# A streaming encoder step on one core: high-weight products first in each tile, and six small moves beside it

## What is computed

```python
x = layer_norm(ALPHA * x + 0.5 * swiglu(x, w_in, w_out))       # two feed-forward parts per layer
# layer 0: S5 mixer. lambda-bar and B-bar from a, dt, b; h[t] = lb * h[t-1] + bb @ u[t]
y = einsum(c_re, hs_re) - einsum(c_im, hs_im) + d_skip * u       # "outputs" of the state space
y = gelu(y) @ w_glu; y = y[:D] * sigmoid(y[D:])
# layer 1: k, v = x @ w_kv (before the layer), q = x @ w_q, rotary on k and q, masked softmax(q k) v, @ w_o
x = layer_norm(ALPHA * x + y)
x = layer_norm(ALPHA * x + 0.5 * swiglu(x, w_in2, w_out2))
```

## Time and profile before

| | |
|---|---|
| time, median of 3 runs | 2318.58 us (2316.3 to 2318.84) |
| the profiled execution | 2318.47 us, its span 2316.7 us |
| PE busy | 97% of the span |
| DVE, ACT, POOL busy | 65%, 50%, 25% |

### The profile page before, as it was taken

How to read it: one execution, slowest core, us unless ns; L and a number is a source line. 1 busy time by engine, 2 the same in 40 slices (tenths; PEclk the granted TensorE clock), 3 DMA queues, 4 the chain that set the end, 5 groups by cost and what they waited for, 6 DMA issues and landing times.

```text
span 2316.7 us, 42670 instructions
## 1 busy us (share of the span) xinstructions
PE 2242.5 (97%) x17171; PEld 2202.2 (95%) x17171; DVE 1516.4 (65%) x2276; ACT 1153.7 (50%) x1939; POOL 572.5 (25%) x491
## 2 busy tenths in 40 slices
PE   8989999999998999999999999999999999999997
PEld 8988999999998998999999999999999999999997
DVE  6898768657788577444474575656687665475444
ACT  4434543565744558433364465555466564354332
POOL 2267401123211342211251123011352011132110
PEclk9999999999999999999999999999999999999998
DMA  9568675454765455555569655544556456455452
GB/s 252 167 194 234 194 218 179 121 171 139 215 213 173 137 166 155 182 151 150 146 201 284 191 162 169 155 121 138 152 156 183 131 149 189 115 153 169 143 157 79
DMA packets 705366, 391.13 MB, mean 169 GB/s; under 512 B 25001, under 2 KB 693138, under 8 KB 705170
## 3 DMA queue, kind: packets, MB, share of 16 engines
q1 hardware_dynamic: 662720, 332.44, 50.1%
q10 hardware_dynamic: 42450, 55.96, 7.3%
HBM read 366.53 MB, written 21.82 MB: 168 GB/s over the span
## 4 chain that ended last, share of the span: by engine, by line
PE 75%; DVE 8%; ACT 3%; issue 2%; POOL 2%; ACTq 0%; POOLq 0%; DVEq 0%
PE tile_ps L542 22%; PE tile_ps L543 22%; PE tile_ps L544 22%; DVE wl L520 2%; PE misc L1749 1%; PE misc L1729 1%; ACT wh L514 1%; PE misc L2109 1%; POOL zq L886 1%; PE misc L2134 1%; PE misc L2309 1%; DVE hs L1557 1%; PE misc L1746 1%; PE misc L2287 0%; DVE r L978 0%
## 5 line engine op out<-in xcount | busy, mean ns | idle before, releaser
L520 DVE TENSOR_TENSOR wl<-raw,wh 128x1024 fp32r<-128x1024 f32 (+1 forms) x640 | 796.0, 1244 | 443.4 <-ACT wh L514 441.5
L542 PE MATMUL tile_ps<-xh,wh 128*128 128x256 f32 (+1 forms) x3520 | 1050.5, 298 | 23.0 <-DVE wl L520 18.6
L543 PE MATMUL tile_ps<-xl,wh 128*128 128x256 f32 (+1 forms) x3520 | 1033.7, 294 | 0.0
L544 PE MATMUL tile_ps<-xh,wl 128*128 128x256 f32 (+1 forms) x3520 | 1033.6, 294 | 0.0
L514 ACT CAST wh<-raw 128x1024 fp32r<-128x1024 f32 (+1 forms) x640 | 655.2, 1025 | 733.4 <-PE tile_ps L544 723.8
L542 PEld LDWEIGHTS tile_ps<-xh,wh 128*128 128x128 f32 x3520 | 664.7, 189 | 31.3 <-issue 20.3
L543 PEld LDWEIGHTS tile_ps<-xl,wh 128*128 128x128 f32 x3520 | 664.7, 189 | 0.9
L544 PEld LDWEIGHTS tile_ps<-xh,wl 128*128 128x128 f32 x3520 | 664.2, 189 | 0.0
L730 POOL TENSOR_TENSOR hl<-hf,hh 128x256 fp32r<-128x256 f32 (+1 forms) x176 | 243.4, 1383 | 1271.4 <-ACT hh L638 1270.8
L542 PE MATMUL tile_ps<-hh,wh 128*128 128x320 f32 (+1 forms) x1472 | 442.3, 300 | 5.8 <-DVE wl L520 5.6
L543 PE MATMUL tile_ps<-hl,wh 128*128 128x320 f32 (+1 forms) x1472 | 433.5, 294 | 0.0
(11 more groups left out here) (301 smaller groups left out, 1767.2 us busy)
## 6 DMA issues: line engine op xcount, KB each, us to landing
raw<-in_ffn_w_in_dram SPq DMA_DIRECT2D x352, 512.0 KB, 3.9
raw<-in_ffn_w_out_dram SPq DMA_DIRECT2D x128, 448.0 KB, 3.6
raw<-in_ffn_w_out_dram SPq DMA_DIRECT2D x64, 512.0 KB, 3.9
raw<-in_ssm_w_glu_dram SPq DMA_DIRECT2D x32, 512.0 KB, 3.8
raw<-in_attn_w_kv_dram SPq DMA_DIRECT2D x32, 512.0 KB, 4.0
wt<-scr_w ACTq DMA_DIRECT2D x16, 512.0 KB, 4.8
cp<-scr_c ACTq DMA_DIRECT2D x16, 512.0 KB, 4.1
raw<-in_attn_w_q_dram SPq DMA_DIRECT2D x16, 512.0 KB, 3.9
```

The lines of the kernel that those rows point to most:

```text
L520: nc.vector.tensor_tensor(wl[n % WS][:, 0:k, :], raw[n % RAWS][:, 0:k, :], wh[n % WS][:, 0:k, :].bitcast(F32), ALU.subtract).then_inc(w_lo, 1)
L542: nc.tensor.matmul(o, wh[w][:, kk, :], xa, start=kk == 0, stop=False)
L543: nc.tensor.matmul(o, wh[w][:, kk, :], xb, start=False, stop=False)
L544: return nc.tensor.matmul(o, wl[w][:, kk, :], xa, start=False, stop=kk == ROWS[n] - 1)
```

## The change

Six edits. (1) PE opens a tile on `wh` alone, does all rows' products with high weights, then waits for `wl`, then does all rows with low weights; tiles that wait row by row for their input, and the two tiles taken together, keep the old order and wait for `wl` first. (2) The state-space outputs begin a step (a tile) later. (3) The second half of x is copied out of PSUM twice by ACT, to `r` and to `xh`; DVE has no part in it. (4) The powers of lambda begin 40 steps later in the tables' program. (5) The eight `skip` tiles are made by ACT. (6) K/V tiles come in another order, and four V tiles are emptied by DVE.

```diff
-KV_ORDER = "kvvvvkkvvvvkkkkk"
+KV_ORDER = "kvvvvkkkvvvvkkkk"
+V_BY_DVE = 8
...
-            pe.wait_ge(w_lo, n + 1)
+            pe.wait_ge(w_hi, n + 1)
...
         def pe_tile(pe, n, h, hi, lo, ready=None, have=0):
             pe_open(pe, n)
+            if ready is None:
+                for kk in range(ROWS[n]):
+                    pe_row_high(n, h, hi, lo, kk)
+                pe.wait_ge(w_lo, n + 1)
+                for kk in range(ROWS[n]):
+                    mm = pe_row_low(n, h, hi, kk)
+                mm.then_inc(tile_done, 1)
+                return
+            pe.wait_ge(w_lo, n + 1)
...
             pe_open(pe, n)
             pe_open(pe, n + 1)
+            pe.wait_ge(w_lo, n + 2)
...
                 wait(pe, s_r2, d)
+                wait(pe, xh_ready[1], X_IN + d)
...
-        def dve_second(dve):
-            for d in range(DT):
-                dve.wait_ge(s_tpx, d + 1)
-                nc.vector.tensor_copy(r[:, d, CS[1]], misc[:, 3, 0:NT[1]]).then_inc(s_r2, 1)
-                yield from idle(2)
-
         def act_second(act):
             for d in range(DT):
-                yield
-                act.wait_ge(s_r2, d + 1)
-                nc.scalar.copy(xh[1][:, d, :], r[:, d, CS[1]]).then_inc(xh_ready[1], 1)
-                yield
+                act.wait_ge(s_tpx, d + 1)
+                nc.scalar.copy(r[:, d, CS[1]], misc[:, 3, 0:NT[1]]).then_inc(s_r2, 1)
+                nc.scalar.copy(xh[1][:, d, :], misc[:, 3, 0:NT[1]]).then_inc(xh_ready[1], 1)
+                yield from idle(2)
...
             w0, w1 = (tmp[:, 15 + k].rearrange("p (a b) -> p a b", a=2) for k in range(2))
+            yield from idle(5 * DT)
...
-                        V.tensor_scalar(skip[dt % 2][:, :], ident[:, :], vec[:, 96 + dt:97 + dt], None, ALU.mult
-                                        ).then_inc(s_dd, 1)
...
                     inputs(dt, 0)
+                    wait(act, s_tb, 3 * (dt - 1))
+                    nc.scalar.activation(skip[dt % 2][:, :], ident[:, :], ACT.Identity,
+                                         scale=vec[:, 96 + dt:97 + dt]).then_inc(s_dd, 1)
...
         def outputs_at(h, grp):
-            return 12 + (grp + 1) * SCAN[h]
+            return 13 + (grp + 1) * SCAN[h]
...
-                else:
-                    act_v_copy(act, 0, j)
+                elif i < V_BY_DVE:
+                    act_v_copy(act, 0, j)
+                else:
+                    act_hi(act, FIRST["kv"] + i + WS)
...
-                    dve_lo(dve, v_tile(0, j) + WS)
+                    n = v_tile(0, j)
+                    if i >= V_BY_DVE:
+                        dve.wait_ge(tile_done, n + 1)
+                        nc.vector.tensor_copy(vT[:, j, 0:NT[0]], bank(n, 0)).then_inc(drained[n % PSS], 1)
+                    dve_lo(dve, n + WS)
```

More of the change, by code:

```diff
@@ L536, in pe_open, with pe_row_high, pe_row_low @@
                 pe_busy(ps[:, n % PSS, 0:P], BUSY_TILES[n])
-            pe.wait_ge(w_lo, n + 1)
-        def pe_row(n, h, hi, lo, kk):
[L540 to L544, removed]
+            pe.wait_ge(w_hi, n + 1)
+        def pe_row_high(n, h, hi, lo, kk):
+            o, w = ps[:, n % PSS, 0:NT[h]], n % WS
+            nc.tensor.matmul(o, wh[w][:, kk, :], hi[:, kk, 0:NT[h]], start=kk == 0, stop=False)
+            nc.tensor.matmul(o, wh[w][:, kk, :], lo[:, kk, 0:NT[h]], start=False, stop=False)
+        def pe_row_low(n, h, hi, kk):
+            return nc.tensor.matmul(ps[:, n % PSS, 0:NT[h]], wl[n % WS][:, kk, :], hi[:, kk, 0:NT[h]],
+                                    start=False, stop=kk == ROWS[n] - 1)
+        def pe_row(n, h, hi, lo, kk):
+            pe_row_high(n, h, hi, lo, kk)
+            return pe_row_low(n, h, hi, kk)
         def pe_tile(pe, n, h, hi, lo, ready=None, have=0):
             pe_open(pe, n)
+            if ready is None:
+                for kk in range(ROWS[n]):
+                    pe_row_high(n, h, hi, lo, kk)
+                pe.wait_ge(w_lo, n + 1)
[4 more added lines that the diff above has]
+            pe.wait_ge(w_lo, n + 1)
             for kk in range(ROWS[n]):
[L549 to L552, removed]
+                if kk == 0 and n in BUSY_ROWS:
+                    pe_busy(ps[:, n % PSS, 0:P], BUSY_ROWS[n])
+                pe.wait_ge(ready, have + kk + 1)
                 mm = pe_row(n, h, hi, lo, kk)
@@ L1136, in pool_second @@
                 yield
+                pool.wait_ge(s_r2, d + 1)
                 pool_lo(pool, 1, d, X_IN)
@@ L2779, in _ @@
                              paced(together(dve_tables(dve), dve_powers(dve)), TABLES))
-            beside = together(chained(dve_rest(dve), dve_lam(dve)), tables, chained(idle(SECOND), dve_second(dve)),
+            beside = together(chained(dve_rest(dve), dve_lam(dve)), tables,
                               chained(idle(LN0), dve_ln(dve, 0, 0), dve_s5(dve, 0)))
```

## The result

The changed kernel (the reordering and five moves beside it) took 2303.66 us (median of six runs, 2303.04 to 2304.83) against 2317.93 in the same comparison: a ratio of 0.9936 (95% interval 0.9923 to 0.9949), 14.3 us less. I had forecast 2292, 26 us less than before, in a range of 2279 to 2308. The sign and the range held; the gain that I forecast was nearly double the measured one.

What follows compares the result with a forecast made beforehand. PE, busy 97% of the span, was taken as the bound, so only its waits and slow clock could be won. Stretch gains of 16.3, 4.6, 0.75, 0.7, -0.8, 3.9 and 1.3 summed to 26.7 us: 2292 us, range 2279 to 2308.

Steps and rivals of the forecast that it cites:

- The wait for `r` and the slow clock behind it: Near 124:130: ACT copies x at once, so the waits (5.6 us with restarts) and half-pace clock (2.7 us) are won back.
- A fulfilled wait in a tile's middle: Inside each tile, before the low products: costs nothing; a rival (chance 0.05) had a bubble there, break-even at 46 ns a tile.
- 723:765: Half 1, within 600:765: DVE has 1.4 us idle of 42 and sheds nothing, so the end rule gains only 0.75 us.
- Costs at nothing: Mid-tile waits, copies and `skip` tiles on ACT, later powers beside POOL's `zq` adds, V copies on DVE: taken as 0 us.
- my own account: Whole kernel: the forecast's stretch-by-stretch sum, 26.7 us gained, 2292 us, own range 2283 to 2301; chance 0.60.
- rival A: Whole kernel: DVE bounds more, waits return later as `wl` mid-tile, `wh` or `cp`; gain 8 to 14 us; chance 0.22.
- 0:300: First stretch: `wl`, `r` and most `ebuf` waits clear, with slow clock and small gaps; 16.3 us gained.
- `ebuf` waits: Within 82:240: DVE sheds around 17 us, so the first four of five go, 4.0 us; 0.8 given back for POOL.
- A wait for `wl` that is shorter than the 1.81 us of high products vanishes if DVE is only late once: Any plain tile: the high products cover it; if DVE has no idle time, at most 1.8 us per stretch, once.
- the norms at 580 and 2062: Layer norms: `wl` waits there gain 0, as the next link (`xl`, 2.9 us) is late anyway.
- 400:440: Half 0 outputs: a tile of real work before the `hs` wait gains 3.1 us, clock behind it 1.5; sum 4.6.
- the adds (800:816): Half 1: later outputs delay the `zc` adds; 0.86 us of `wl` gained, 1.66 lost, minus 0.8.

## Why the prediction was half right

**Right.** The wait for `r` and the slow clock behind it were there to be had by moves off DVE (edits 3 to 5 alone: 13.5 us in all; the copy alone: 5.8). A fulfilled wait in a tile's middle costs nothing that these runs can tell from zero. The `cp` wait stayed at 1.74. That DVE bounds 723:765 and PE gains little there held: five waits in a tile's middle with 5.7 us, and one for `wh`. Costs at nothing held as well: a `skip` tile on ACT takes 405 ns, where I had worked out an estimated 0.41 from the Trainium skill ("ScalarE: Activation LUTs", Rules for kernel authors); whether moving this multiply off VectorE, against that page's advice, gained anything by itself no run shows. The powers met POOL's `zq` adds as feared: L1330, the changed kernel's number for L1317, took 0.77 us at 250.70, beside an add that started at 250.68, and 0.19 at 254.93 with none beside it, as the Trainium skill has it ("SBUF — State Buffer", Who interferes with whom). It cost PE nothing.

**The range held for another reason than mine.** The time is outside the 2283 to 2301 of my own account (0.60) and at the edge of rival A's 2304 to 2310.5 (0.22), and the range held because it took A in. A's mechanism is also what part of the trace shows: waits that come back for `wh` (4.9 us in four, one of them 1.23 at 199.75 where before had 1.36 for `wl`) and for `wl` in a tile's middle (6.0).

**Stretch by stretch**, the gain forecast, the lead gained by the changed kernel, and that of the same kernel without the reordering, in us:

| stretch | forecast | changed kernel | without the reordering |
|---|---|---|---|
| 0:411 | 16.3 | 9.8 | 9.8 |
| 411:489 | 4.6 | 5.9 | 4.8 |
| 489:623 | 0 | -2.6 | -1.1 |
| 623:789 | 1.45 | -1.6 | -1.7 |
| 789:869 | -0.8 | -1.5 | -1.5 |
| 869:925 | 3.9 | 2.1 | 2.3 |
| 925 to the end | 1.3 | 2.8 | -0.1 |
| sum | 26.7 | 14.9 | 12.5 |

**0:300 was mis-sized, 9.8 us for 16.3.** The changed kernel begins 0.7 us late and is 1.2 late at 62 us, where its `raw` tiles landed later (the first tile starts between 10.2 and 12.4 in the traces); and there a row-waiting tile stands 1.68 for `wl`, which I had let vanish with the plain ones. Of the `ebuf` waits 0.75 and 1.25 stayed where I had 0.8 in all, and the wait at 208.78 only turned from one for `wl` (1.36) into one for `wh` (1.23). The last column says that the reordering had no part in the 9.8, where I had the `wl` waits' 4.2 in good part from it.

**The step that failed** is the sentence "A wait for `wl` that is shorter than the 1.81 us of high products vanishes if DVE is only late once". The wait vanishes where it stood. But where what comes next is a product that waits for something else from DVE or POOL (`r`, `hs`, `zq`), PE just arrives there earlier and stands the same time in one piece. I had reasoned so for the norms at 580 and 2062 and set them to 0, and had not asked what one long wait does to the clock that two short ones do not. Measured: the reordering alone gives -9.5 us, with PE's gaps as long as before, and filling alone brings 10.6 back; on top of the other edits it gives +1.2. I priced clock only as something that comes back. The table shows where: in 400:440, where the later outputs stand in the way of the gathered wait, the sum held (5.9 for 4.6, and 4.8 of it comes without the reordering); at the norm in 489:623, set to 0, the changed kernel lost 1.5 more than without the reordering. The pace of the last section took 1.7 there and gave 0.8 back, with the reordering and without. By the medians edits 2, 1 and 6 added to 3 to 5 give 0.9 us (2304.55 to 2303.66), less than either median's spread, where I had 10.4; by the leads behind 411 us it is 5.1.

**Missed altogether:** in half 1 the outputs in their old place had been covering a late `wl`. Before, output products stood where the tile of 688.20 now stands open for 3.69 us, and the stretch around them loses 1.6 us with the reordering, 1.7 without it, and nothing with edits 3 to 5 alone, whose outputs keep their place. Moving cover is a loss where the cover was; I priced the shift at the adds (800:816) and not there. At the adds, 0.8 of a loss was 1.5, and not by the wait that I named: the wait for `zc` became shorter (0.88 for 1.52), and a new one of 1.13, for the gelu's `xl`, stands ahead of it.

**Open:** the four microseconds between the lead of edits 3 to 5 in their trace and in their median; what the `skip` tiles gave; whether edit 6 is worth its 2.4 us; and why the clock fell behind 1.92 us of waiting at 731 in the changed kernel and not behind 2.56 at 1745, nor behind 2.60 at 739 in the kernel before. I give no rule for it.

## What to carry to other kernels

Letting the busiest engine start a tile on half its operand only helps if nothing else that it waits for is late from the same producer; otherwise waits add up to one, and on TensorE a long one often costs twice, the wait and the half-speed stretch behind. So first take work off the producer (here 13.5 us from three small moves), then reorder (here up to 5.4 more, once the row-waiting tiles took part), and put real work or filling matmuls where the gathered wait will stand. Test each edit alone and with the rest: here one was worth -9.5 alone and +1.2 in company, another 0.6 alone and 8.7 in company.

## What the runs showed of the hardware

The same 256-column tile matmuls run at one of two paces at full clock. For the same tiles, with no wait in the stretch, the busy table of before (490:530) and of the kernel with only the outputs moved:

```profile
490.00:530.00 40.00, 40.00 (x355) 40.00 (x354) 23.52 (x29) 18.46 (x25) 5.84 (x7) 1.00 0.65 187
```

```profile
490.00:530.00 40.00, 40.00 (x342) 40.00 (x341) 22.35 (x29) 16.83 (x22) 4.44 (x6) 1.00 0.64 181
```

355 against 342 matmuls in 40 us, 113 and 117 ns apart. The pace can hold over many tiles in a row, as it does here. It is not fixed by the program: the changed kernel and the one with the K/V edit undone have the same program until near 840 us, and in 18:28, at full clock and without a wait, their traces have

```profile
18.00:28.00 10.00, 10.00 (x87) 10.00 (x87) 5.49 (x6) 4.35 (x8) 2.94 (x2) 1.00 0.95 249
```

```profile
18.00:28.00 10.00, 10.00 (x91) 10.00 (x90) 5.70 (x6) 4.56 (x8) 2.94 (x2) 1.00 1.01 262
```

87 matmuls in the first and 91 in the second. Over the whole span the mean start distance at 256 columns was 115.4 ns before and 115.7 in the changed kernel, 2.2 us for some 7,110 such matmuls. What sets the pace the runs don't show; a part of the difference between two traces, or two runs, of one kernel can be this.
